# Gathering expert rows by one native fp32 product instead of a high and a low part, with two more weight buffers

## The reference, cut to what matters

```
def expert_choice_ffn(h, w_router, w_gate, w_up, w_down):
    B_, L, D = h.shape                                   # 1, 512, 1024
    cap = EC_CAPACITY * L // N_EXPERTS                   # 64 rows for each of 16 experts
    aff = softmax(h @ w_router)
    top_aff, top_idx = lax.top_k(swapaxes(aff, 1, 2), cap)
    xe = jax.vmap(lambda hb, ib: hb[ib])(h, top_idx)     # the gather: rows of h by expert
    hid = silu(einsum('becd,edf->becf', xe, w_gate)) * einsum('becd,edf->becf', xe, w_up)
    ye = einsum('becf,efd->becd', hid, w_down) * top_aff[..., None]
    return combine(top_idx, ye)                          # scattered back and added
```

## Time and profile before

| | |
|---|---|
| median of 3 runs | 2615.38 us |
| the profiled execution: its time | 2614.52 us |
| its span, first to last instruction | 2612.7 us |
| TensorE busy | 2498.3 us, 96% |
| VectorE / ScalarE / GpSimd busy | 1254.7 / 740.1 / 160.1 us |
| mean granted TensorE clock | 0.989 |

### The profile page before, as it was taken

The page is one execution under the profiler, slowest core; times in us unless marked ns, Lnnn a source line. Parts: engine busy times, 40 slices in busy tenths (PEclk is TensorE's granted clock), DMA queues, the critical chain, the costliest instruction groups (busy, mean ns, idle before and its releaser), DMA issues.

```text
span 2612.7 us, 34135 instructions
## 1 busy us (share of the span) xinstructions
PE 2498.3 (96%) x14650; PEld 1679.0 (64%) x14650; DVE 1254.7 (48%) x1979; ACT 740.1 (28%) x1170; POOL 160.1 (6%) x102
## 2 busy tenths in 40 slices
PE   8999999999999999999999999999999979999996
PEld 4446677788886435677788888777899533444332
DVE  5964446533344985364633434595655332112122
ACT  2243343421222144243422322536212130111001
POOL 0000000000000000000000000361233010000000
PEclk9999999999999999999999999999999989999999
DMA  4334212224323224321332433210000439999997
GB/s 161 93 117 173 97 49 78 70 82 120 97 72 132 61 97 162 101 93 33 100 105 78 113 87 99 91 65 33 3 3 3 193 147 412 421 421 421 421 422 303
DMA packets 243389, 380.60 MB, mean 146 GB/s; under 512 B 21769, under 2 KB 182822, under 8 KB 218534
## 3 DMA queue, kind: packets, MB, share of 16 engines
q1 hardware_dynamic: 242876, 378.08, 40.3%
q10 hardware_dynamic: 362, 0.33, 0.0%
HBM read 376.28 MB, written 2.10 MB: 145 GB/s over the span
## 4 chain that ended last, share of the span: by engine, by line
PE 81%; DVE 8%; DMA 7%; ACT 3%; issue 1%; SPq 0%; DVEq 0%; ACTq 0%
PE banks L1076 34%; PE banks L1010 9%; PE banks L1934 9%; PE banks L1646 3%; PE banks L1484 3%; PE banks L1059 2%; PE banks L1778 2%; DMA ring<-in_w_gate 2%; DMA arena<-in_w_gate 2%; DVE arena L2842 2%; PE banks L1115 1%; PE banks L1355 1%; PE banks L1063 1%; PE banks L1329 1%; DMA ring<-in_w_down 1%
## 5 line engine op out<-in xcount | busy, mean ns | idle before, releaser
L2207 ACT ACTIVATE w_hi<-ring 128x2048 fp32r<-128x2048 f32 (+1 forms) x100 | 174.7, 1747 | 423.9 <-PE banks L1076 423.9
L2718 DVE TENSOR_TENSOR w_lo<-ring,w_hi 128x2048 fp32r<-128x2048 f32 (+1 forms) x96 | 198.7, 2069 | 128.7 <-ACT w_hi L2207 127.5
L1076 PE MATMUL banks<-ffn_x_hi,w_hi 128*128 128x512 f32 x640 | 249.0, 389 | 0.0
L1076 PE MATMUL banks<-ffn_x_lo,w_hi 128*128 128x512 f32 x640 | 249.0, 389 | 0.0
L1076 PE MATMUL banks<-ffn_x_hi,w_lo 128*128 128x512 f32 x640 | 249.0, 389 | 0.0
L2842 DVE SCALAR_TENSOR_TENSOR arena<-arena,taps 128x512 f32<-128x512 f32 x240 | 166.1, 748 | 2.5
L3054 DVE TENSOR_TENSOR squares<-gates,banks 128x512 f32<-128x512 f32 x44 | 30.3, 688 | 275.7 <-PE banks L1076 262.4
L1010 PE MATMUL banks<-xT,ring 128*128 128x512 f32 x320 | 139.1, 594 | 0.5 <-ACT taps L2073 0.5
L1076 PE MATMUL banks<-ffn_hidden_hi,w_hi 128*128 128x512 f32 x352 | 138.4, 393 | 0.0
L1076 PE MATMUL banks<-ffn_hidden_hi,w_lo 128*128 128x512 f32 x352 | 137.1, 389 | 0.0
L1076 PE MATMUL banks<-ffn_hidden_lo,w_hi 128*128 128x512 f32 x352 | 137.0, 389 | 0.0
(11 more groups left out here) (474 smaller groups left out, 4446.1 us busy)
## 6 DMA issues: line engine op xcount, KB each, us to landing
ring<-in_ffn_w_in SPq DMA_DIRECT2D x88, 512.0 KB, 5.1
ring<-in_w_down SPq DMA_DIRECT2D x30, 1024.0 KB, 24.7
arena<-in_w_gate SPq DMA_DIRECT2D x29, 1024.0 KB, 24.4
arena<-in_w_up SPq DMA_DIRECT2D x29, 1024.0 KB, 23.6
ring<-in_w_gate SPq DMA_DIRECT2D x26, 1024.0 KB, 23.3
ring<-in_w_up SPq DMA_DIRECT2D x26, 1024.0 KB, 24.0
arena<-in_w_down SPq DMA_DIRECT2D x26, 1024.0 KB, 26.0
ring<-in_w_mod SPq DMA_DIRECT2D x24, 1024.0 KB, 7.3
```

Of the source, the lines that this page charges most:

```text
L1076: mm = pe.matmul(bank[:, :], weights(wp, k), rhs(rp, k), start=(k == 0 and wp == rp), stop=(k == n - 1 and wp == 1))
L2207: nc.scalar.activation(hi[:, 0:m], raw[n % 2][:, 0:m], ACT.Copy).then_inc(f_hi.sem, 1)
L2718: ins = V.tensor_tensor(lo[:, 0:m], raw[n % 2][:, 0:m], hi[:, 0:m].bitcast(F32), ALU.subtract)
```

## The change

`h_tok` becomes one fp32 tensor, where the low part was. ScalarE writes each piece once, GpSimd's eight subtractions go, and `gather` does 4 fp32 products for each half instead of 8 fp32r products, with the same 0/1 matrix read as fp32. The 16 KB on each partition that held the high part become two more buffers of the weight ring, so `EB` is 16; they are loaded behind the output projection like chunks 10 and 11 (there is no wait of its own for them), and the two buffers in `xT` are now numbers 14 and 15. Two more semaphores are reused.

```
-        h_tok = [rounded("h_tok_hi", arena_at + 4 * mix2_at, ST, D), rounded("h_tok_lo", arena_at + 4 * qT_at, ST, D)]
...
-        h_full = view(qT_at, ST, D)
+        h_tok = view(qT_at, ST, D)
...
-        ht_mm, ht_ev, ht_lo = sem("h_turned"), sem("h_high"), sem("h_low")
+        ht_mm, ht_ev = sem("h_turned"), sem("h_by_token")
...
-        E_IN_BEFORE = [..., (rows_in, DEPTH * 17 * 16)] + [(s, DEPTH * 16 * SPLIT_CHUNKS) for s in raw_in]
+        E_IN_BEFORE = [..., (rows_in, DEPTH * 17 * 16), (ctx_loaded, 16), (up_in.sem, DEPTH * 64)] + [(s, DEPTH * 16 * SPLIT_CHUNKS) for s in raw_in]
...
-        e_w += ring_now[2:6] + [xT.rearrange("p a n -> p (a n)")[:, i * EC:(i + 1) * EC] for i in range(2)]
+        e_w += ring_now[2:6] + [view(mix2_at + i * EC, EC) for i in range(2)] + [xT.rearrange("p a n -> p (a n)")[:, i * EC:(i + 1) * EC] for i in range(2)]
         EB = len(e_w)
-        E_GATE, E_DELTA, E_HEADS, E_OUT, E_X = 0, 2, 7, 8, 12
+        E_GATE, E_DELTA, E_HEADS, E_OUT, E_X = 0, 2, 7, 8, 14
...
                 if n >= 6:
-                    pe.wait_ge(ht_ev, 2 * (n - 5))
+                    pe.wait_ge(ht_ev, n - 5)
...
                 if n < 6:
-                    pe.wait_ge(ht_ev, 2 * (n + 3))
+                    pe.wait_ge(ht_ev, n + 3)
...
-                for i in range(2 * ST):
-                    t, part = i // 2, h_tok[i % 2]
-                    mm = pe.matmul(aux.bank(f"G{hf}", q), selq[:, t].rearrange("p j c -> p (j c)"),
-                                   part[:, t, hf * 512:(hf + 1) * 512], start=(i == 0), stop=(i == 2 * ST - 1))
+                for t in range(ST):
+                    mm = pe.matmul(aux.bank(f"G{hf}", q), selq[:, t].rearrange("p j c -> p (j c)").bitcast(F32),
+                                   h_tok[:, t, hf * 512:(hf + 1) * 512], start=(t == 0), stop=(t == ST - 1))
                 mm.then_inc(ax_mm, 1)
...
-            pe.wait_ge(ht_lo, 2 * ST)
+            pe.wait_ge(ht_ev, 2 * ST)
...
             def by_token(n):
                 act.wait_ge(ht_mm, n + 1)
-                for dst in (h_tok[0], h_full):
-                    A1(dst[:, n // 2, (n % 2) * 512:(n % 2 + 1) * 512], ps[2 + n % 6][:, :], ACT.Copy).then_inc(ht_ev, 1)
+                A1(h_tok[:, n // 2, (n % 2) * 512:(n % 2 + 1) * 512], ps[2 + n % 6][:, :], ACT.Copy).then_inc(ht_ev, 1)
...
-            for n in range(2 * ST):
-                pool.wait_ge(ht_ev, 2 * (n + 1))
-                cols = slice((n % 2) * 512, (n % 2 + 1) * 512)
-                G.tensor_tensor(h_tok[1][:, n // 2, cols], h_full[:, n // 2, cols], h_tok[0][:, n // 2, cols].bitcast(F32),
-                                ALU.subtract).then_inc(ht_lo, 1)
```

More of the change, by code:

```diff
@@ L582, in build @@
         e_used = sem("expert_chunk_used")
-        E_IN_BEFORE = [(rope_v, 10), (rope_s, 2), (p2_mm, 2), (cond_ok, 2), (const_in, 32), (x_in[0], 16), (x_in[1], 16), (mem_in, 16), (turned, 12), (turned_out, 12), (rows_in, DEPTH * 17 * 16)] + [(s, DEPTH * 16 * SPLIT_CHUNKS) for s in raw_in]
+        E_IN_BEFORE = [(rope_v, 10), (rope_s, 2), (p2_mm, 2), (cond_ok, 2), (const_in, 32), (x_in[0], 16), (x_in[1], 16), (mem_in, 16), (turned, 12), (turned_out, 12), (rows_in, DEPTH * 17 * 16), (ctx_loaded, 16), (up_in.sem, DEPTH * 64)] + [(s, DEPTH * 16 * SPLIT_CHUNKS) for s in raw_in]
         ex_silu, ex_hid = sem("expert_silu"), sem("expert_hidden")
```

## The result

The changed kernel takes 2623.67 us (median of 9 runs, 2621.39 to 2627.27), beside 2616.47 for the kernel before (9 runs, 2614.11 to 2617.29). The ratio is 1.0028, with a 95% interval of 1.0018 to 1.0038: slower, by 7.2 us. Forecast was 2621.9, slower by 6.5. Of the 1.8 us between the two times, 1.1 is the median before, which nine runs put at 2616.47 and the first three at 2615.38.

A forecast was written before the change was run, and what follows sets the result against it. The stream sets the end before the change, TensorE after it: 21.7 + 3.0 - 0.5 us of extra TensorE work exceeds its 17.7 us slack by 6.5, so 2615.38 + 6.5 = 2621.9 us, range 2614.5 to 2626.5.

The forecast's parts named there:

- The bound changes hands: At the last weight chunk: TensorE replaces the stream as what sets the end, its extra 24.2 us going 6.5 beyond the slack.
- The slack of 17.7 us: Before the change, TensorE alone could begin the last weight chunk at 2573.8 us, but the trace has 2591.54.
- the undisturbed pair: Expert pair with TensorE alone in the chain of waits, 55.15 us per pair, repeated to build TensorE's own schedule.
- Seven gathers inside the pairs: Gathers within the expert pairs: native fp32 products add 3.1 us each to TensorE, +21.7 us in all.
- The first gather: Gather ahead of all pairs, at a low clock: 9.0 us against 6.07, so +3.0 us; bounds +0.9 to +7.6.
- ScalarE's copy: Ahead of the routing: one copy fewer on the chain moves all that follows forward, -0.5 us; the seven others bring nothing.
- Two more buffers: Weight ring: 176 chunks to bring instead of 178, -5.0 us on the stream's end, which no longer sets the time.
- A sign that was wrong: Late stages of the changed profile: the stream would run below 421 GB/s because it waits for buffers.
- The stream as bound: Rival at the kernel's end: the stream still ends last and the buffers pay, -2.5 us, to 2612.9; chance 0.16.
- Starving at every gather: Rival in the pairs: the stream stands still up to 3.1 us at each gather, time 2625 to 2632; chance 0.10.
- The late clock: Rival at the first gather: clock rises late, up to +4.6 us more, 2626.5; three quarters of a 0.08 chance.

The follow-up runs named there:

- kernel with products that last to the gather: Changed kernel plus 11 products of no use filling TensorE's idle time and one more right before the first gather: 2622.26 us, 1.0021.
- two pairs of kernels where the stream sets the end: Kernel before, against it without the two xT buffers (2621.39 us); changed kernel with one-part fp32r gather, 16 buffers (2610.74 us) against 14 (2617.26).

## Why the prediction was right

**The bound changes hands.** This was the step on which all hung, and it held. No transfer is in the chain of the changed kernel, and without the two buffers it is as fast. The slack of 17.7 us, built from the undisturbed pair, comes out of the trace of the changed kernel as well: TensorE's extra work is 22.0 + 3.65 - 0.4 = 25.3 us, and the last chunk is 7.4 us later, which leaves 17.9.

**Seven gathers inside the pairs.** +3.14 us each (58.29 - 55.15), 22.0 in all, against 3.1 and 21.7. The shape in the output projection was the right row to take the price from: 7.06 there, 7.07 here. Its upper bound with a cost for changing the kind of product was too careful.

**The first gather.** The mechanism held, the size was off: +3.65 us against +3.0. I took the clock to rise after the same 4.4 us as before, and it rose about 5.3 us after the gather's start (changed kernel, by stages):

```profile
2131.10:2135.50 4.40, 4.39 (x5) 1.83 (x6) 0.00 (x0) 0.00 (x0) 0.00 (x0) 0.50 0.00 0
2135.50:2136.50 1.00, 1.00 (x3) 0.47 (x2) 0.00 (x0) 0.00 (x0) 0.00 (x0) 0.56 0.00 0
2136.50:2140.80 4.30, 4.30 (x11) 1.59 (x9) 0.00 (x0) 0.60 (x1) 0.00 (x0) 1.00 0.00 0
```

The kernel with products that last to the gather (7.12 us) shows that the clock is all there is to it, apart from the native price. Its 0.65 us is as large as the 0.7 between forecast and result; the pairs' 0.3 and the copy's 0.1 are offset in part by the slack, which came out 0.2 larger.

**ScalarE's copy.** -0.4 against -0.5: the first gather starts 56.6 us after the projection's start, not 57.0. The seven other copies and GpSimd's work brought nothing, as forecast.

**Two more buffers.** They were requested at 2098.48 and 2098.96, behind loads of the output projection's end, and cost nothing. The stream's last bytes move by 2594.5, 520.0 us after the projection's start. The forecast had 517.0 (2589.1), at worst 520.1, so it came out at the late end, still 6.8 us ahead of TensorE's last chunk. The buffers pay 0 here, and 5.7 and 6.5 us in the two pairs of kernels where the stream sets the end, where the forecast price was 5.0.

**A sign that was wrong.** I wrote that the stream would fall below 421 GB/s in the late stages, as it would wait for buffers. It ran at 421 to 2520 us and beyond. My own numbers said so: at 58.25 us per pair against 59.7 TensorE is still the faster one in each pair, the stock of loaded chunks shrinks, and the stream always has a free buffer. TensorE sets the end because the stock outlasts the run (that of 14 does too), not because it is slower per pair. Both are at full rate to the end.

**Rivals.** The stream as bound falls by the chain of waits and by the kernel without the buffers. Starving at every gather falls by the 421 GB/s of the late stages. The 358 GB/s that a rule gives for loads from HBM (the Trainium skill, DMA: Bandwidth & Descriptors, "Where 436 GB/s comes from") is again not what this stream shows, at 421. The late clock was the rival with something in it, at 0.65 us and not 4.6.

## What to carry to other kernels

When two resources are both near full, measure the slack of each at the end before trading one for the other. Here TensorE had 17.7 us to give and was asked for 25. The buffers that were bought with it pay only while the stream is last. A high and a low part in a shorter type can give the space of one full copy and keep the cheap products. Shorter work in a stretch of low clock is only a gain if the clock does not stay low for what comes behind it; look at where it rises, and at the next stretches too.

## What the runs showed of the hardware

- In native fp32 one product of 128 x 128 x 512 costs 0.88 us at 2.4 GHz (7.07 for eight), two fp32r products 0.49 (3.92 for sixteen), two bfloat16 products no more than 0.45 (3.40 for a chain piece of 15 records).
- TensorE's clock did not follow the work in the short term: with TensorE idle from 2124.7 to 2128.0 the granted share was still 0.94, and behind it 0.50. With gaps of no more than 0.91 us from there to the gather it stayed at 1.00. A first gather cut from 6.09 to 3.77 us did not bring the first reload forward (68.3 us against 67.8), as the work behind it ran at the low level instead: the clock rose some 12 us after the gather's start, against 4.4.
- The clock also fell behind the waits for the hidden row: in the first pair of every trace, for some 3.4 us in nine of them and 6.8 in four, and in the last expert of three of thirteen, for some 3.5 us, where 16 records took 5.35 us instead of 3.65 in two of them.
